# The opening of a hybrid decoder layer: the first block's products wait operand by operand, GpSimd adds three of the squares, TensorE multiplies zeros first

## The reference

```
def rmsnorm(x, g):
    xf = x.astype(jnp.float32)
    y = xf * lax.rsqrt(jnp.mean(xf * xf, axis=-1, keepdims=True) + EPS)
    return (y * g.astype(jnp.float32)).astype(x.dtype)
...
    proj = hn @ w_in.astype(hn.dtype)
```

## Time and profile before

| | |
|---|---|
| median of 3 runs | 2068.93 us (2068.31 to 2069.67) |
| profiled execution, its own time | 2070.8 us |
| its span | 2069.0 us |
| PE busy | 2034.7 us (98%) |
| DVE busy | 1176.3 us (57%) |
| ACT busy | 626.6 us (30%) |
| POOL busy | 287.4 us (14%) |

### The profile page before, as it was taken

The page is one execution under the profiler, slowest core; times in us unless marked ns, Lnnn a source line. Parts: engine busy times, 40 slices in busy tenths (PEclk is TensorE's granted clock), DMA queues, the critical chain, the costliest instruction groups (busy, mean ns, idle before and its releaser), DMA issues.

```text
span 2069.0 us, 30409 instructions
## 1 busy us (share of the span) xinstructions
PE 2034.7 (98%) x12940; PEld 1949.7 (94%) x12940; DVE 1176.3 (57%) x1357; ACT 626.6 (30%) x794; POOL 287.4 (14%) x275
## 2 busy tenths in 40 slices
PE   8999999999999999999999999999999999999998
PEld 8999998999999999999999999999999999999996
DVE  6457565566667656566433343466565656565656
ACT  5223334434333444344443332211111111111113
POOL 0000003758370222222000002000000000000002
PEclk9999999999999999999999999999999999999999
DMA  9235666654555754645153221111011101110102
GB/s 281 93 103 136 142 158 202 187 191 154 163 154 133 173 177 137 187 146 156 60 186 109 88 70 51 62 61 52 31 51 51 52 31 51 52 53 31 60 31 82
DMA packets 252204, 227.11 MB, mean 110 GB/s; under 512 B 141102, under 2 KB 209622, under 8 KB 251942
## 3 DMA queue, kind: packets, MB, share of 16 engines
q1 hardware_dynamic: 252070, 225.17, 36.0%
HBM read 161.29 MB, written 63.84 MB: 109 GB/s over the span
## 4 chain that ended last, share of the span: by engine, by line
PE 91%; DVE 3%; ACT 2%; DMA 2%; issue 2%; SPq 1%; POOL 0%; POOLq 0%; DVEq 0%; ACTq 0%
PE a_psum L895 33%; PE a_psum L145 31%; PE a_psum L1164 11%; PE a_psum L882 5%; PE a_psum L970 1%; PE a_psum L988 1%; PE a_psum L1071 1%; PE a_psum L998 1%; PE a_psum L952 1%; PE a_psum L1014 1%; DMA w_raw<-in_w_in 1%; PE a_psum L967 1%; PE a_psum L1086 1%; PE a_psum L1094 1%; PE a_psum L1085 1%
## 5 line engine op out<-in xcount | busy, mean ns | idle before, releaser
L895 PE MATMUL a_psum<-xh,w_hi 128*128 128x342 f32 (+3 forms) x1656 | 535.6, 323 | 3.9 <-DVE w_lo L1515 3.9
L895 PE MATMUL a_psum<-xl,w_hi 128*128 128x342 f32 (+3 forms) x1656 | 531.4, 321 | 0.0
L895 PE MATMUL a_psum<-xh,w_lo 128*128 128x342 f32 (+3 forms) x1656 | 529.7, 320 | 0.0
L895 PEld LDWEIGHTS a_psum<-xh,w_hi 128*128 128x128 f32 x1656 | 312.2, 189 | 7.1 <-DVE w_lo L1515 4.5
L895 PEld LDWEIGHTS a_psum<-xl,w_hi 128*128 128x128 f32 x1656 | 312.3, 189 | 1.0
L895 PEld LDWEIGHTS a_psum<-xh,w_lo 128*128 128x128 f32 x1656 | 312.2, 189 | 0.0
L1218 ACT ACTIVATE w_hi<-w_raw 128x1024 fp32r<-128x1024 f32 x125 | 132.0, 1056 | 433.1 <-PE a_psum L145 409.5
L1293 ACT ACTIVATE post<-a_psum 128x342 f32<-128x342 f32 (+3 forms) x207 | 94.7, 457 | 554.2 <-PE a_psum L895 518.5
L145 PE MATMUL a_psum<-xh,w_hi 128*128 128x342 f32 (+1 forms) x1152 | 245.1, 321 | 9.2 <-DVE xl L1537 9.2
L1515 DVE TENSOR_TENSOR w_lo<-w_raw,w_hi 128x1024 fp32r<-128x1024 f32 x125 | 156.6, 1253 | 159.6 <-ACT w_hi L1218 159.6
L145 PE MATMUL a_psum<-xl,w_hi 128*128 128x342 f32 (+1 forms) x1152 | 245.1, 321 | 0.0
(11 more groups left out here) (239 smaller groups left out, 2807.8 us busy)
## 6 DMA issues: line engine op xcount, KB each, us to landing
w_raw<-in_w_in SPq DMA_DIRECT2D x76, 512.0 KB, 3.7
w_raw<-in_w_up SPq DMA_DIRECT2D x44, 512.0 KB, 3.5
mix_scratch<-post SPq DMA_DIRECT2D x32, 522.0 KB, 2.8
down_raw<-in_w_ffn_down SPq DMA_DIRECT2D x22, 512.0 KB, 4.3
ext<-mix_scratch SPq DMA_DIRECT2D x9, 1024.0 KB, 6.9
y<-mix_scratch SPq DMA_DIRECT2D x18, 512.0 KB, 5.5
ext<-grow_scratch SPq DMA_DIRECT2D x9, 512.0 KB, 5.5
ext<-mix_scratch SPq DMA_DIRECT2D x9, 512.0 KB, 6.8
```

The costliest lines, as they stand in the source:

```text
L895: mm = pe.matmul(psum[:, u % 2, 0:n], w[:, k, :], x[:, k, at0:at0 + n], start=(k == 0 and part == 0), stop=(k == KC - 1 and part == 2))
```

## The change

Four things change, all within the first 30 us. TensorE runs seven products of zeros as soon as `zero` is cleared. The nine products of block 0 wait for each kind of operand apart, and come in another order (high by high, high input by low weight, low input by high weight). On ScalarE block 0 of `xh` is made in three pieces, and each square comes one place later, behind the next block's `xh`. GpSimd adds the squares 0, 1 and 2 into `post[5]`, and VectorE makes five sums in place of seven, behind more of the `xl` blocks.

```
@@ -906,7 +909,23 @@
-                    pe.wait_ge(w_lo, 1)
+
+                    def first_block(s):
+
+                        def products(j, w, x, start):
+                            pe.matmul(psum[:, 2 + 3 * s + j, 0:N3], w[s][:, 0, :], x[:, 0, N3 * j:N3 * j + N3], start=start,
+                                      stop=False)
+
+                        pe.wait_ge(w_hi, s + 1)
+                        for j in range(3):
+                            pe.wait_ge(x_hi, j + 1)
+                            products(j, wh, xh, True)
+                        pe.wait_ge(w_lo, s + 1)
+                        for j in range(3):
+                            products(j, wl, xh, False)
+                        pe.wait_ge(x_split, 1)
+                        for j in range(3):
+                            products(j, wh, xl, False)
...
+                    pe.wait_ge(zero_set, 1)
+                    for n in range(7):
+                        pe.matmul(psum[:, 0, 0:256], zero[:, 0:P], zero[:, 0:256], start=True, stop=True)
+                    first_block(0)
+                    first_block(1)
+                    for k in range(1, KC // 2):
                         first_two(0, (k,))
-                        if k == 0:
-                            pe.wait_ge(w_lo, 2)
                         first_two(1, (k,))
                     first_two(0, range(KC // 2, KC))
                     pe.wait_ge(consts_in, 16)
-                    pe.wait_ge(d_xss, KC - 1)
+                    pe.wait_ge(d_xss, 5)
@@ -1229,15 +1252,22 @@
+                    def square_in(k):
+                        if k >= 4:
+                            act.wait_ge(*((summed, 1), (summed, 1), (summed, 2), (d_xss, 1))[k - 4])
+                        act.activation(post[k % 4][:, :], y[:, k, :], ACT.Square).then_inc(a_xsq, 1)
...
-                        act.activation(xh[:, k, :], y[:, k, :], ACT.Copy, scale=par[:, PAR_N1 + k:PAR_N1 + k + 1]
-                                       ).then_inc(x_hi, 1)
+                        for cols in [slice(N3 * j, N3 * j + N3) for j in range(3)] if k == 0 else [slice(0, T)]:
+                            act.activation(xh[:, k, cols], y[:, k, cols], ACT.Copy, scale=par[:, PAR_N1 + k:PAR_N1 + k + 1]
+                                           ).then_inc(x_hi, 1)
                         if k == 0:
                             split_high(1)
-                        if k >= 4:
-                            act.wait_ge(d_xss, k - 4 if k > 4 else 1)
-                        act.activation(post[k % 4][:, :], y[:, k, :], ACT.Square).then_inc(a_xsq, 1)
+                        else:
+                            square_in(k - 1)
+                    square_in(KC - 1)
@@ -1525,23 +1555,25 @@
+                        dve.wait_ge(*((a_xsq, 5), (a_xsq, 6), (a_xsq, 7), (summed, X_SUMS), (a_xsq, KC))[n])
...
-                        if k > 1:
-                            sum_squares(k - 1)
-                    sum_squares(KC - 1)
+                        if k > 4:
+                            sum_squares(k - 5)
+                    sum_squares(3)
+                    sum_squares(4)
@@ -1973,6 +2005,11 @@
             pool.memset(zero, 0.0).then_inc(zero_set, 1)
+            pool.wait_ge(a_xsq, 2)
+            pool.tensor_tensor(post[5][:, :], post[0][:, :], post[1][:, :], ALU.add).then_inc(summed, 1)
+            pool.wait_ge(a_xsq, 3)
+            pool.wait_ge(summed, 1)
+            pool.tensor_tensor(post[5][:, :], post[5][:, :], post[2][:, :], ALU.add).then_inc(summed, 1)
```

More of the change, by code:

```diff
@@ L108 @@
 Q_EPS = EPS * P * P
+X_SUMS = 2
 def shape_constants():
@@ L916, in first_two @@
                                 mm.then_inc(units_done, 3)
-                    for k in range(KC // 2):
+                    pe.wait_ge(zero_set, 1)
[4 more added lines that the diff above has]
+                    for k in range(1, KC // 2):
                         first_two(0, (k,))
-                        if k == 0:
-                            pe.wait_ge(w_lo, 2)
                         first_two(1, (k,))
@@ L1139, in _ @@
             pe.wait_ge(h_added, KC)
-            pe.wait_ge(summed, KC - 1)
+            pe.wait_ge(summed, X_SUMS + KC - 1)
             for b in range(3):
@@ L1446, in _ @@
                 if m >= 3:
-                    act.wait_ge(summed, m - 2)
+                    act.wait_ge(summed, X_SUMS + m - 2)
                 act.activation(sq[m % 2] if m else ssq, res[:, m, :], ACT.Square).then_inc(squared, 1)
@@ L1526, in _, with sum_squares @@
                     dve.wait_ge(params_in, 16)
-                    def sum_squares(k):
-                        dve.wait_ge(a_xsq, k + 1)
-                        if k > 1:
-                            dve.wait_ge(d_xss, k - 1)
-                        dve.tensor_tensor(post[4][:, :], post[4][:, :] if k > 1 else post[0][:, :], post[k % 4][:, :],
-                                          ALU.add).then_inc(d_xss, 1)
+                    def sum_squares(n):
+                        dve.wait_ge(*((a_xsq, 5), (a_xsq, 6), (a_xsq, 7), (summed, X_SUMS), (a_xsq, KC))[n])
+                        if n:
+                            dve.wait_ge(d_xss, n)
+                        dve.tensor_tensor(post[4][:, :], post[4][:, :] if n else post[3][:, :],
+                                          post[(0, 1, 2, 5, 3)[n]][:, :], ALU.add).then_inc(d_xss, 1)
                     for k in range(KC):
-                        dve.wait_ge(x_hi, k + 1)
+                        dve.wait_ge(x_hi, k + 3)
                         dve.scalar_tensor_tensor(out=xl[:, k, :], in0=y[:, k, :], scalar=par[:, PAR_N1 + k:PAR_N1 + k + 1],
@@ L1579, in _ @@
                     for k in range(KC):
-                        dve.wait_ge(x_hi, KC + k + 1)
+                        dve.wait_ge(x_hi, KC + k + 3)
                         dve.wait_ge(normed, k + 1)
@@ L2056, in _ @@
                 if m > 1:
-                    pool.wait_ge(summed, m - 1)
+                    pool.wait_ge(summed, X_SUMS + m - 1)
                 pool.tensor_tensor(ssq, ssq, sq[m % 2], ALU.add).then_inc(summed, 1)
```

## The result

The changed kernel takes 2073.90 us (median of 21 runs, 2071.11 to 2076.85), the kernel before, run beside it, 2069.67 us (21 runs, 2067.33 to 2072.71). The ratio is 1.0020, its 95% interval 1.0015 to 1.0026: slower by 4.2 us (3.1 to 5.4). The profiled execution took 2071.92 us, with a span of 2070.1.

The account below looks back on a forecast made before the run. TensorE, nearly gapless, was bound at the column sums by its own chain and VectorE's. GpSimd's additions would delay these sums 3.1 us with nothing absorbing it: 2068.93 becomes 2072.1 us, range 2068.4 to 2074.6.

Parts of the forecast that it names:

- the likeliest case: Opening: GpSimd's additions hold VectorE, column sums start later, +2.5 to +3.6 us, 2071.2 to 2073.0; chance 0.62.
- rival (a): TensorE's gap before the column sums also lowers its clock, 1.7 us more, 2073.8; chance 0.14.
- Two chains meet at the column sums: At about 28.6 us TensorE's work and VectorE's sums meet; the later sets the start, so both must become earlier.
- the most that TensorE's side can bring: TensorE's early start alone would reach the column sums at 26.1, 2.5 us earlier.
- The start: TensorE's opening: zeros from 1.68 end by 7.7, real products find full clock or get it soon, at no cost.
- Whole turns between GpSimd and VectorE: In the opening, two-input VectorE instructions and GpSimd's additions lock one shared port; the second waits for the whole first.
- The order of the sums: VectorE's opening: three sums instead of two behind the last `xl`, ending at 28.8, 0.3 us late without the lock.
- The size of the turns: GpSimd's 2.6 us additions end at 16.7 and 20.6, moving the running sum's end to 31.7, column sums +3.1 us.
- Rival (b): Opening: GpSimd's additions hardly hold VectorE; sums end at 28.8, +0.3 us, 2069.2; chance 0.15.
- (c): Opening: sums are no wait, TensorE's early start pays its own 2.5 us, 2066.4; chance 0.09.
- (d): Zeros do not bring full clock; block 0's 18 matmuls cost 2.4 us more, time stays; no chance of its own.
- Nothing behind them takes it up: Behind the column sums no later work absorbs their delay, so the 3.1 us reach the total.

Follow-up runs that it names:

- kernel 1: The changed kernel without GpSimd's additions, VectorE making all seven sums in the old places; 2070.43 against 2069.37 us, ratio 1.0005.
- kernel 8: The kernel before with only the seven products of zeros added; 2070.91 us, ratio 1.0005.
- kernel 5: The changed kernel with all sums on VectorE and the column sums behind more of TensorE's products; 2067.77 against 2070.22 us, ratio 0.9988.
- kernel 2: The kernel before with only GpSimd's additions and the new order of the sums; 2071.64 us, ratio 1.0009.
- kernel 6: The changed kernel with a third GpSimd addition of the same width, whose result nothing reads; 2076.63 us, ratio 1.0030.
- kernel 3: The changed kernel without the seven products of zeros; 2072.93 us, ratio 1.0016.
- kernel 7: The changed kernel with four more products of zeros ahead of the wait for the sums; 2072.45 us, ratio 1.0011.
- kernel 4: The changed kernel with the column sums two blocks later in TensorE's queue; 2070.56 us, ratio 1.0004.
- kernel 9: Kernel 5 without the seven products of zeros; 2068.18 against 2070.12 us, ratio 0.9991.
- kernel 12: The kernel before with 28 waits for the cleared `zero` ahead of TensorE's first product, no zero products; 2069.58 against 2070.51 us, ratio 0.9999.

## Why the prediction held

It gave 2072.1 us for a kernel before of 2068.93, so +3.1; +4.2 (3.1 to 5.4) was measured, and 2073.90 lies in its range. By the bound of 0.2% the result is at the edge. It lies above the likeliest case's own range (2071.2 to 2073.0), and next to the 2073.8 of rival (a), so the time alone would speak for that rival; the traces decide. The mechanism came as forecast. That the number fits so well is in part luck: the opening of the first trace took 1.05 us less than the 3.1 given, and the other 2.2 of the 4.2 us are not in that opening; the prediction's sum had nothing for them.

- **Two chains meet at the column sums: right.** Kernels 1 and 8 gave TensorE its lead without the additions, and it ended in waits of 0.90 and 0.89; kernel 5 took the meeting point away and won 2.6 us in the opening. The 2.5 us given as the most that TensorE's side can bring was right, but for an order of the queue that the changed kernel doesn't have.
- **The start: right.** Zeros end at 6.98 (by 7.7), first product 7.00, full clock by 8.13. The three pieces of `xh` took 1.54 against 1.17 for one, 0.37 where I took 0.3, and it was hidden: the next instruction of ScalarE started at 7.71 as before.
- **Whole turns between GpSimd and VectorE: right in kind.** Shown from both sides (kernels 1 and 2) and by dose (kernel 6). The rule that the prediction named from the Trainium skill (SBUF — State Buffer, SBUF: two separate sides) agrees with these rows: `xl` 3 and 4 stretch to 2.71 and 3.48 us beside an addition each, and `xl` 5, without one, takes 1.29. The order of the sums was priced at 0.3 us without the lock and is worked out above at 0.1.
- **The size of the turns: 1.1 us too much in all.** Addition 1 was in by 13.63, not 14.1, because `xl` 2 ran 0.2 earlier and the addition's recorded start lies inside it; it ended at 16.25 for 16.7. Addition 2 ended at 19.65 for 20.6: it holds VectorE 2.2 us (9.51 - 7.33), not its 2.6. From there the pieces are as forecast, 10.9 us for 11.1. The sums ended at 30.58 for 31.7, and the opening lost 2.05 for 3.1.
- **Rival (a), the clock, is real in part of the executions.** It fell behind the gap in one of three traces, and in kernel 6; in kernel 3, with a gap of 2.25, it did not. The price given, 1.7 us, is what it took (40.50 - 38.81 of kernel 7, whose column sums start at the same 31.09, is 1.69). I held it back as an alternative; it is an addition that comes now and then, 0.6 us on average if one in three holds, which three traces can't settle.
- **Rival (b)** falls with 7.33 us for three `xl`, **(c)** with the wait of 2.26, **(d)** with 0.63 from 8.13.
- **"Nothing behind them takes it up": right for the opening, but the prediction put what the rest adds at nothing.** Two readings show that it adds something. The first is the clock. The record has the mean granted clock of each execution, to three digits. It is 0.9966 on average in the 21 of the changed kernel and 0.9974 in 97 of the kernel before beside the experiments (one more there, at 0.947 with an ordinary time, is left out). The difference, 0.0008 of 2070 us, is about 1.7 us by this estimate, and with the opening's 2.05 it makes 3.75 of the 4.2. (It is at the high end: a slower TensorE also waits less at the next place, as at 703 us.) Within the changed kernel the 11 executions at 0.996 took 2074.9 us on average, the 8 at 0.997 2072.8 and the 2 at 0.998 2071.7. Which part of the change lowers the clock is not shown: kernels 3 (no zeros) and 4 (no gap at the sums) have 0.9966 and 0.9965 as well, kernels 1, 2 and 8, each with a part of the change, 0.9969 to 0.9971, and kernels 9 and 12 0.9977.
- **The second is the load at 680 us.** From the start of tile 2 to the matmuls behind that wait it is 650.6 us on average in the five traces without zeros (649.9 to 650.9) and 651.6 in the nine with them (649.5 to 653.2). These 1.0 us are taken ahead of the wait at 703 us, which is shorter or missing where TensorE comes late. To the end of the span it is 2031.4 us without zeros (2029.7 to 2032.6) and 2032.8 with them (2031.4 to 2034.3), so something like it remains, in ranges that overlap.

What the traces show, beside the measured times: opening (tile 2 less 36.39), and the same plus 1.0 where a kernel has the zeros. A fall of the clock in the opening is in the first, those behind it are in neither.

| kernel | opening | with the 1.0 | measured |
|---|---|---|---|
| changed, mean of three traces | +2.8 | +3.8 | +4.1 |
| 1, no additions | -0.1 | +0.9 | +1.0 |
| 2, additions alone | +1.4 | +1.4 | +1.9 |
| 3, no zeros | +2.4 | +2.4 | +3.3 |
| 4, column sums later | -0.2 | +0.8 | +0.8 |
| 5, both | -2.6 | -1.6 | -2.5 |
| 6, third addition | +6.1 | +7.1 | +6.2 |
| 7, zeros in the gap | +2.4 | +3.4 | +2.3 |
| 8, zeros alone | 0.0 | +1.0 | +1.0 |
| 9, kernel 5 without zeros | -1.9 | -1.9 | -1.9 |
| 12, waits for zeros | +0.2 | +0.2 | -0.2 |

"Measured" is the ratio less one, times 2070. Each has 1 to 2 us of uncertainty to either side, so the table can refute a large missing term but not prove the small one. All eleven agree within 1.1 us. But the 1.0 is not what makes them agree: without it kernels 5, 6 and 7 fit within 0.1, and the changed kernel and kernels 1, 4 and 8 are 1.0 to 1.3 short. So the table bears out the opening, and not the size of the rest.

The profiled execution of the changed kernel was only 1.1 us above that of before, with an opening 2.05 later. The difference does not come from the clock between 684 and 720 us: one trace has its fall behind 690.61, the other behind 703.20, where the changed one doesn't wait, and the product that starts at 720.09 in the kernel before starts at 722.28 in the changed one, 2.2 later. The 1.1 went in smaller steps behind that, the scatter of single executions.

Left open: why the load at 680 us lands later in kernels with zeros, and why the changed kernel runs for longer at half clock behind the opening. The traces show when the load lands and not what holds it. A version with the full 28 entries and no products would go on from here; it was not tried.

## What to carry to other kernels

An instruction moved to an idle engine isn't free when that engine takes turns with the one that is late: price it by the time for which the other is held, 2.2 us here for a sum that VectorE makes in 1.2. Before taking work off the later of two chains, look at what asks for its result: moving the asker behind products that were ready (kernel 4) undid the loss of 2.05 us against the kernel before, and with the sums left on VectorE (kernel 5) it made the early start worth 2.6 us. An early start alone pays nothing as long as a later wait ends at the same time.

## What the runs showed of the hardware that I had not expected

- The granted clock fell to half behind a wait of 2.25 us in one execution and not in two others with waits of 2.24 and 2.26, at the same place of the same program. The same gap is no sure cost and no sure safety; where it fell it took 1.7 us. Nor is a shorter wait safe: in kernel 2 TensorE waited 1.28 us at 680 and then ran 16 passes of 32 columns in 1.97, and the two stretches of 2 us from 690 have 0.67 and 0.50, while the wait of 1.27 in the earlier trace rows had no fall behind it.
- GpSimd's addition holds VectorE for less (2.2 us) than its record is long. Records of the additions that queue behind an `xl` are 3.25 to 3.44 us, those that get in first 2.6: the longer ones hold some waiting.
- A transfer at 680 us landed 7.8 to 9.0 us behind its issue in nine traces with the zeros, and 7.4 to 7.5 in five without. Zero products as a warm-up are cheap where they stand, but the rest of the program was not the same behind them.
